# Pacing the loads of the first chunk by the landing of earlier units, and splitting its second unit in halves

## The reference

```python
u = rms_norm(h, norm_mix_g[i])
mix = nsa_mixer(u, nsa_w_in[j], ...)          # 16 heads of 128, 4 key/value groups
h = h + mix
u = rms_norm(h, norm_mlp_g[i])
h = h + jnp.square(jax.nn.relu(u @ mlp_w1[i])) @ mlp_w2[i]      # 2048 -> 8192 -> 2048
gate = jax.nn.sigmoid(rms_norm(h, ple_norm_g[i]) @ ple_w_gate[i])
h = h + gate * (p[i] @ ple_w_proj[i])
```

## Time and profile before

| | us |
|---|---|
| median of 3 runs (lowest, highest) | 1208.8 (1207.68, 1210.01) |
| profiled execution | 1206.92 |
| its span | 1204.8 |
| PE busy | 1194.7 (99%) |
| PE weight loads busy | 992.3 (82%) |
| DVE busy | 729.9 (61%) |
| ACT busy | 591.7 (49%) |
| POOL busy | 70.6 (6%) |

### The profile page before, as it was taken

The page is one execution under the profiler, slowest core; times in us unless marked ns, Lnnn a source line. Parts: engine busy times, 40 slices in busy tenths (PEclk is TensorE's granted clock), DMA queues, the critical chain, the costliest instruction groups (busy, mean ns, idle before and its releaser), DMA issues.

```text
span 1204.8 us, 15261 instructions
## 1 busy us (share of the span) xinstructions
PE 1194.7 (99%) x5504; PEld 992.3 (82%) x5504; DVE 729.9 (61%) x956; ACT 591.7 (49%) x812; POOL 70.6 (6%) x63
## 2 busy tenths in 40 slices
PE   8999999999999999999999999999999999999998
PEld 7888788888888888888888888888888888888886
DVE  5676646778766656554465554555555557476554
ACT  7655444666656554443444433445433444455443
POOL 1000000000000011100011100011000012000000
PEclk9999999999999999999999999999999999999999
DMA  9766564333348666765567765677755676785661
GB/s 348 283 210 217 176 202 135 118 106 106 112 152 267 221 222 217 248 226 195 193 211 260 237 207 192 190 242 236 241 192 196 207 242 221 248 263 194 217 206 49
DMA packets 107278, 247.02 MB, mean 205 GB/s; under 512 B 9424, under 2 KB 52432, under 8 KB 107216
## 3 DMA queue, kind: packets, MB, share of 16 engines
q1 hardware_dynamic: 107072, 246.24, 62.5%
q10 hardware_dynamic: 144, 0.01, 0.0%
HBM read 232.58 MB, written 13.63 MB: 204 GB/s over the span
## 4 chain that ended last, share of the span: by engine, by line
PE 94%; DVE 2%; ACT 1%; DMA 1%; SPq 1%; issue 0%; ACTq 0%
PE acc L1425 87%; PE sc L1566 1%; DMA x_raw<-in_x_cols_dram 1%; DVE w_split L947 1%; PE tr L1483 1%; ACT s L698 1%; PE sc L1531 0%; PE tr L1472 0%; PE sc L1472 0%; PE tr L1617 0%; PE tr L1618 0%; SPq L365 0%; PE acc L1455 0%; PE tr L1595 0%; ACT q_split L683 0%
## 5 line engine op out<-in xcount | busy, mean ns | idle before, releaser
L947 DVE TENSOR_TENSOR w_split<-w_raw,w_split 128x1024 fp32r<-128x1024 f32 x411 | 509.7, 1250 | 382.6 <-ACT w_split L597 382.1
L597 ACT ACTIVATE w_split<-w_raw 128x1024 fp32r<-128x1024 f32 x411 | 432.0, 1058 | 419.9 <-PE acc L1425 415.3
L1425 PE MATMUL acc<-w_split,a_hi 128*128 128x512 f32 x1916 | 594.5, 391 | 3.1 <-DVE w_split L947 3.1
L1425 PE MATMUL acc<-w_split,b_split 128*128 128x512 f32 x1920 | 441.0, 390 | 0.0
L1425 PEld LDWEIGHTS acc<-w_split,a_hi 128*128 128x128 f32 x1916 | 356.4, 188 | 78.3 <-issue 4.1
L1425 PEld LDWEIGHTS acc<-w_split,b_split 128*128 128x128 f32 x1920 | 359.4, 188 | 74.0
L1425 PE MATMUL acc<-w_split,a_lo 128*128 128x512 f32 x958 | 373.2, 390 | 0.0
L1425 PEld LDWEIGHTS acc<-w_split,a_lo 128*128 128x128 f32 x958 | 179.9, 188 | 37.7
L562 POOL TENSOR_TENSOR stage<-stage 128x512 f32<-128x512 f32 x32 | 49.8, 1574 | 559.1 <-ACT stage L605 559.1
L698 ACT ACTIVATE s<-s,nmx,q_scale 128x128 f32<-128x128 f32 (+1 forms) x64 | 34.2, 539 | 6.4 <-DVE nmx L1114 6.4
L605 ACT ACTIVATE stage<-acc,rstd 128x512 f32<-128x512 f32 x48 | 30.1, 678 | 10.1 <-PE acc L1425 9.6
(11 more groups left out here) (185 smaller groups left out, 515.9 us busy)
## 6 DMA issues: line engine op xcount, KB each, us to landing
w_raw<-in_mlp_w_units_dram SPq DMA_DIRECT2D x256, 512.0 KB, 4.3
w_raw<-in_nsa_w_in_units_dram SPq DMA_DIRECT2D x79, 512.0 KB, 4.3
w_raw<-in_nsa_w_out_units_dram SPq DMA_DIRECT2D x32, 512.0 KB, 3.7
w_raw<-in_ple_w_gate_units_dram SPq DMA_DIRECT2D x32, 512.0 KB, 4.2
turn_dram<-junk SPq DMA_DIRECT2D x44, 128.0 KB, 4.1
turn_dram<-s SPq DMA_DIRECT2D x44, 128.0 KB, 4.1
v_slc<-turn_dram SPq DMA_DIRECT2D x22, 256.0 KB, 4.0
v_win<-turn_dram SPq DMA_DIRECT2D x22, 256.0 KB, 4.4
```

Of the source, the lines that this page charges most:

```text
L597: nc.scalar.activation(w_hi[:, u % SPLIT], w_raw[:, u % RAW], ACT.Copy).then_inc(hi_done, 1)
L947: nc.vector.tensor_tensor(w_lo[:, u % SPLIT], w_raw[:, u % RAW], f32(w_hi[:, u % SPLIT]), ALU.subtract).then_inc(lo_done, 1)
L1425: last = nc.tensor.matmul(acc[c % 2][t][:], xs[:, kt, toks], ws[:, u % SPLIT, m * NW:(m + 1) * NW], start=(kt == 0 and n == 0), stop=(kt = ...
```

## The change

In the first chunk SP waits, ahead of the x columns of unit k, for k of 2 to 7, until the weights of unit k - 2 have landed. Unit 1 is loaded in two halves of 256 KB onto two semaphores, and ACT, DVE and PE treat it in halves as they do unit 0. `first_full` becomes a list, and the half steps become functions. PE runs 8 fillers instead of 10.

```diff
+HALVED = 2
-        first_full = sem("first_full")
+        first_full = [sem(f"first_full{u}") for u in range(HALVED)]
...
                     if c == C_KC:
                         kts = slice(UNIT_KT * k, UNIT_KT * (k + 1))
+                        if k >= 2:
+                            sp.wait_ge(raw_full[u - 2], 16)
                         sp.dma_start(x_raw[:, kts], x_cols[:, kts]).then_inc(x_cols_full[k - 1], 16)
+                    if u < HALVED:
+                        for m, full in enumerate((first_full[u], raw_full[u])):
+                            sp.dma_start(slot(u)[:, m], packed(w_in_units, col // NW, k)[:, m]).then_inc(full, 16)
+                        continue
                     load(u, packed(w_in_units, col // NW, k), slot(u))
...
+            def first_half(u):
+                act.wait_ge(first_full[u], 16)
+                nc.scalar.activation(w_hi[:, u, 0:NW], w_raw[:, u, 0:NW], ACT.Copy).then_inc(first_hi, 1)
...
-                    if isinstance(i, int) and u == 0:
-                        act.wait_ge(raw_full[0], 16)
-                        nc.scalar.activation(w_hi[:, 0, NW:UW], w_raw[:, 0, NW:UW], ACT.Copy).then_inc(hi_done, 1)
+                    if isinstance(i, int) and u < HALVED:
+                        if u:
+                            first_half(u)
+                        act.wait_ge(raw_full[u], 16)
+                        nc.scalar.activation(w_hi[:, u, NW:UW], w_raw[:, u, NW:UW], ACT.Copy).then_inc(hi_done, 1)
...
+            def first_half(u):
+                dve.wait_ge(first_hi, u + 1)
+                nc.vector.tensor_tensor(w_lo[:, u, 0:NW], w_raw[:, u, 0:NW], f32(w_hi[:, u, 0:NW]),
+                                        ALU.subtract).then_inc(first_lo, 1)
...
-                if m == 0 or kt == 1 and c == C_KC:
+                if c == C_KC and k < HALVED and m == 0:
+                    pe.wait_ge(first_lo, u + 1)
+                elif m == 0 or c == C_KC and k < HALVED:
                     pe.wait_ge(lo_done, u + 1 + 8 * UPC * i)
...
-            keep_busy(10)
+            keep_busy(8)
```

More of the change, by code:

```diff
@@ L424, in _ @@
                     if u == 0:
-                        for m, full in enumerate((first_full, raw_full[0])):
+                        for m, full in enumerate((first_full[0], raw_full[0])):
                             sp.dma_start(x_raw[:, m], x_cols[:, m]).then_inc(first_x[m], 16)
@@ L726, in _ @@
             x_part(0, (0,))
-            act.wait_ge(first_full, 16)
-            nc.scalar.activation(w_hi[:, 0, 0:NW], w_raw[:, 0, 0:NW], ACT.Copy).then_inc(first_hi, 1)
+            first_half(0)
             x_part(0, (1,))
@@ L940, in split_lo @@
                     u = first + k
+                    if isinstance(i, int) and 0 < u < HALVED:
+                        first_half(u)
                     dve.wait_ge(hi_done, u + 1 + 8 * UPC * i)
-                    if isinstance(i, int) and u == 0:
-                        nc.vector.tensor_tensor(w_lo[:, 0, NW:UW], w_raw[:, 0, NW:UW], f32(w_hi[:, 0, NW:UW]),
+                    if isinstance(i, int) and u < HALVED:
+                        nc.vector.tensor_tensor(w_lo[:, u, NW:UW], w_raw[:, u, NW:UW], f32(w_hi[:, u, NW:UW]),
                                                 ALU.subtract).then_inc(lo_done, 1)
@@ L1187, in _ @@
             x_part(0, (0,))
-            dve.wait_ge(first_hi, 1)
-            nc.vector.tensor_tensor(w_lo[:, 0, 0:NW], w_raw[:, 0, 0:NW], f32(w_hi[:, 0, 0:NW]),
-                                    ALU.subtract).then_inc(first_lo, 1)
+            first_half(0)
             x_part(0, (1,))
```

## The result

The changed kernel takes 1210.88 us (median of 15 runs, 1209.47 to 1212.62) against 1208.32 us (15 runs, 1206.79 to 1210.01) before: ratio 1.0023, 95% interval 1.0016 to 1.0030. It is slower by 2.6 us as the medians have it (1.9 to 3.6 us by the interval). The forecast was no change, 1208.6 us with a range of 1206.4 to 1210.4; the time lies above it, nearest to rival B (1211.7).

What follows compares the result with a forecast made beforehand. The prediction took PE, busy 99% of the span, as the bound, with the start of unit 7 setting the end. Its terms, 0.0 - 0.2 + 0.0 us, gave a median of 1208.6 us, range 1206.4 to 1210.4.

Steps and rivals of the forecast that it cites:

- rival B: First chunk: DMA engines run dry between units 2 and 4, three uncovered first-byte delays, 2.9 us, 1211.7 us; chance 0.10.
- who sets 28.86: PE's start of unit 7, at 28.86 us: set by its x columns landing at about 24.07, ready 4.64 us later.
- Part 1: Unit 1 in halves: PE starts it 1.82 us earlier but gives all back at units 2 and 7; gain 0.0 us.
- Part 2, the lower end: Waits in SP's queue: two units in flight leave 0.9 us to spare; cost 0, or up to 0.95 us a group.
- Part 2, the upper end: Waits in SP's queue: unit 1 complete at 7.8 instead of 9.64, up to 1.8 us gained; 0.2 taken.
- rival A: Held-back loads did take bandwidth: all first-chunk landings come up to 1.8 us earlier, 1207.0 us; chance 0.22.
- Part 3: Two fillers fewer at the start: PE could start about 0.5 us earlier, nothing comes of it; cost 0.0 us.
- A PE at the lower clock: Slower matmuls at unit 1 after fewer fillers: 1.3 us there, covered by the wait at unit 7, so cost 0.0.

Runs made afterwards that it cites:

- e1: The changed kernel without the waits in SP's queue (unit 1 in halves and 8 fillers stay): 1208.55 us, ratio 1.0005 to the kernel before.
- e2: The kernel before with the six waits alone: 1210.53 us, ratio 1.0016.
- e6: The kernel before with 8 fillers instead of 10 and nothing else: 1207.79 us, ratio 1.0003.
- e3: The changed kernel with waits one unit looser, three units under way instead of two: 1208.16 us, ratio 1.0005 to the kernel before.
- e4: The changed kernel with the waits only ahead of units 2, 3 and 4: 1211.54 us, ratio 1.0025 to the kernel before.
- e5: The changed kernel with the waits only ahead of units 5, 6 and 7: 1209.31 us, ratio 1.0011 to the kernel before.
- e14: The changed kernel with each wait behind its unit's x columns, ahead of the weights: 1209.72 us, ratio 1.0019 to the kernel before.
- e10: The kernel before with ACT's sums one unit later and nothing else: 1207.44 us, ratio 0.9993.
- e8: The changed kernel without waits, with ACT's sums of x one unit later: 1207.35 us, ratio 0.9988 to the kernel before.
- e12: The kernel before with units 1 and 2 halved, sums one unit later, x quarters issued behind units 7 to 10: 1205.99 us, ratio 0.9982.
- e13: The changed kernel, all waits kept, x quarters issued behind units 2 to 5 instead of 4 to 7: 1210.63 us, ratio 1.0020 to before.

## Why the prediction was wrong

**What bounds the kernel, and who sets 28.86: right.** The delay of the columns of unit 7 (2.55 us) is the delay of unit 7 (2.56) and, within its interval, of the whole (0.0023 x 1208.3 = 2.8 us, 1.9 to 3.6).

**Part 1: right.** e1 shows each place within 0.3 us, though PE's first idle time lay elsewhere: 1.15 us ahead of the second half of unit 0 and 0.19 at unit 1, instead of 0.73 at unit 1. In the change itself PE started unit 1 even earlier, at 9.77.

**Part 2, the lower end: wrong, and this is the step that failed.** The prediction put it so: "So there is 0.9 us to spare", "Cost: 0, and if the cover is gone, up to 0.95 us a group". It compared the first-byte delay of an empty queue (0.95 us) with the time in which a unit passes (1.85 us), as if all 16 DMA engines came to the end of a unit together and kept their full rate until then. The measured cost is 2.55 us. e2 shows that the waits alone make the loss, e1 and e6 that nothing else does, and e3 that one more unit under way gives 396 GB/s back: at a depth at which the prediction counted 0.9 us to spare, the transfers had already lost a fifth of their rate (314 instead of 404 GB/s). The same section had the fact that should have warned: when unit 1 was complete, more bytes had been moved than belonged to it, so some engines must have been well past it, while SP waits for the last one. An engine ahead has less queued than the count by units says. That fits the fall before SP's issue at 11.23, but it is argued, not shown: no run here made the engines even, and e4, e5 and e14 (above) don't follow from it.

**Part 2, the upper end (rival A): about what was taken, in the change.** The weights of unit 1 landed earlier, by 8.75 instead of 9.64, but in e1, without any wait, PE starts unit 1 within 0.2 us of the same time (9.96, 9.77). With unit 1 whole the profile with waits has it 0.7 to 1.1 us earlier (e2 against before, e6 and e10). All landings of the chunk coming earlier, which rival A needed, was not seen: from unit 3 on they came later.

The Trainium skill's rule, "DMA: Bandwidth & Descriptors", section "Queues, rings and completion order" (each engine takes one queue's descriptors in ring order), spoke against a gain, and in the runs the landings came in the order of issue. The prediction drew from it that later loads can't delay earlier ones. No run here shows that: e1 agrees within 0.2 us at PE, while in e2, where later loads were held back, unit 1 landed 0.7 to 1.1 us earlier, for a reason that one profile doesn't settle.

**Part 3: right for the sum** (e6: 1.0003). A PE at the lower clock, which it priced at up to 1.3 us, did occur, but not through the fillers: in three of the profiled executions the granted clock fell after PE's idle time, in e8 to 0.50, and one of the three (e10) has all ten fillers.

**Rivals and chances.** B was the outcome, at 0.10. Its price, 3 x 0.95 = 2.9 us on the columns, was close to the 2.55 measured, but partly by luck. The transfers did not stop three times for the first-byte delay; they ran at 314 GB/s for 8 us. The waits of units 5 to 7, free in B, cost something (e5), and in e4 the low rate outlasted the last wait. The chance was far too low, because the one number for the first byte came from an idle queue and nothing in the trace before showed the rate of a shallow queue. The 204 GB/s from 4 to 6 are no such number: at 4.09 some 1.2 MB were issued and not yet moved (1.83 issued, 0.58 moved by 4).

**What stays open.** That the six waits cause the loss, by making the x columns of unit 7 late, is shown. Why the transfers run slower is not. The low rate has two parts which these runs don't separate: the DMA share falls from 1.04 to 0.94 between 8 and 16, a tenth, and the bytes per unit of share fall from 388 to 334, a seventh (404/1.04 and 314/0.94). Idle engines would give the first; why busy ones move fewer bytes is not shown. Nor is why e14, with more queued than the change, is hardly better, or why in e4, with fewer waits and 2.0 to 2.5 MB queued after the last one, the rate stays at 294 GB/s.

## What to carry to other kernels

Holding the queue engine until an earlier load has landed can slow all the transfers, even when by the mean time of a transfer there is time to spare: here two units of 768 KB under way were too little (314 GB/s), three were enough (396). Before shortening a wait, follow the consumer to its next wait and ask what stands behind that; here 2 us won at unit 1 were lost at unit 7 (e1), and the kernels that gained moved the work ahead of unit 7 as well (e8, e12). And when a count of queued bytes says that there is cover, try one load more under way before trusting it: runs with the same count differed by over 60 GB/s (e13, e14).

## What the runs showed of the hardware

An idle time of PE of 2 to 2.5 us is sometimes followed by half the clock and sometimes not. After 2.55 us (before) and 2.02 us (after) the granted clock stayed at 1.00; after 2.54 us (e10) it was 0.59 in the window from 12 to 14, after 2.20 us (e8) 0.50 from 10 to 12, after 2.28 us (e4) 0.61 from 16 to 20. In e10 that made one unit 1.6 us longer. It hits single executions of one kernel: of 33 runs of the kernel before on one chip, the nine with a mean granted clock of 1.000 took 1207.30 us on average, the four with 0.996 or 0.997 took 1209.85. So a profile can show a start that is 1 to 2 us off what the median says. Whether closing such a gap is worth more than its length was not measured.
